# Final norm of a hybrid decoder layer on one core: the work of its last loop divided anew over VectorE, ScalarE and GpSimd

## What is computed

```python
def rmsnorm(x, g):
    xf = x.astype(jnp.float32)
    y = xf * lax.rsqrt(jnp.mean(xf * xf, -1, keepdims=True) + NORM_EPS)
    return (y * g.astype(jnp.float32)).astype(x.dtype)
...
# x: the residual stream, D_MODEL = 1024 wide; each token adds two weighted expert outputs,
# and the result goes through rmsnorm(x, final_norm_g)
```

## Time and profile before

| what | value |
|---|---|
| median of three runs | 1878.3 us |
| the profiled execution's own time | 1877.61 us |
| its span, first to last instruction | 1875.9 us |
| busy share of the span: PE, DVE, ACT, POOL | 88%, 35%, 20%, 10% |
| last expert step's scatter issued | 1824.90 us |
| first add of the last loop | 1833.22 us |
| last multiply of the last loop issued | 1872.33 us |

### The profile page before, as it was taken

How to read it: one execution, slowest core, us unless ns; L and a number is a source line. 1 busy time by engine, 2 the same in 40 slices (tenths; PEclk the granted TensorE clock), 3 DMA queues, 4 the chain that set the end, 5 groups by cost and what they waited for, 6 DMA issues and landing times.

```text
span 1875.9 us, 21634 instructions
## 1 busy us (share of the span) xinstructions
PE 1657.0 (88%) x8136; PEld 1060.9 (57%) x8136; DVE 661.6 (35%) x1238; ACT 369.1 (20%) x653; POOL 189.2 (10%) x297
## 2 busy tenths in 40 slices
PE   5999889999599989989989999999999758968960
PEld 3666556776277767767767775666445733323320
DVE  2003039734444343343433531677112311101117
ACT  3100230021113223133231325100012111101102
POOL 2003500002110110101101010000000001101100
PEclk9999979979699999999999999999999569989985
DMA  4111101109111111101111112265201076675646
GB/s 155 34 35 43 37 12 35 44 11 96 59 33 44 42 44 44 46 31 42 49 39 46 46 56 84 94 255 204 81 34 57 1 314 250 244 292 181 218 163 271
DMA packets 38072, 181.21 MB, mean 97 GB/s; under 512 B 5401, under 2 KB 5721, under 8 KB 29025
## 3 DMA queue, kind: packets, MB, share of 16 engines
q1 hardware_dynamic: 21808, 113.94, 17.7%
q0 software_dynamic: 16176, 66.01, 10.9%
HBM read 336.75 MB, written 38.21 MB: 200 GB/s over the span
## 4 chain that ended last, share of the span: by engine, by line
PE 83%; DMA 6%; DVE 5%; issue 3%; ACT 2%; SPq 0%; POOL 0%; DVEq 0%; ACTq 0%; POOLq 0%
PE ps L447 34%; PE ps L829 7%; PE ps L775 7%; PE ps L744 6%; PE ps L843 3%; DMA arena<-in_w_gu 3%; PE ps L689 3%; PE ps L603 2%; PE ps L598 2%; PE ps L581 2%; PE ps L608 2%; DMA scr<-h_rows,idx 1%; PE ps L497 1%; PE ps L790 1%; PE ps L465 1%
## 5 line engine op out<-in xcount | busy, mean ns | idle before, releaser
L447 PE MATMUL ps<-arena,wring 128*128 128x344 f32 x2304 | 699.6, 454 | 1.2 <-ACT arena L925 1.2
L447 PEld LDWEIGHTS ps<-arena,wring 128*128 128x128 f32 x2304 | 426.1, 190 | 205.5 <-issue 7.3
L829 PE MATMUL ps<-arena,scr 128*32 128x512 f32 x1280 | 152.1, 628 | 23.9 <-DMA arena<-in_w_gu 23.9
L1669 POOL DMA_DIRECT2D gate_scratch<-stage x96 | 52.0, 542 | 803.1 <-ACT stage L978 544.6
L775 PE MATMUL ps<-arena 128*128 128x512 f32 (+1 forms) x288 | 125.6, 594 | 1.2 <-DVE arena L1437 1.2
L744 PE MATMUL ps<-arena,wring 128*128 128x344 f32 x384 | 111.2, 451 | 0.0
L829 PEld LDWEIGHTS ps<-arena,scr 128*32 128x32 f32 x1280 | 41.6, 115 | 120.0 <-issue 102.4
L744 PEld LDWEIGHTS ps<-arena,wring 128*128 128x128 f32 x384 | 72.5, 189 | 38.6
L843 PE MATMUL ps<-arena,scr 128*32 128x512 f32 x640 | 77.6, 628 | 15.0 <-issue 13.6
L775 PEld LDWEIGHTS ps<-arena 128*128 128x128 f32 (+1 forms) x288 | 50.7, 178 | 71.0 <-issue 69.2
L886 ACT ACTIVATE arena<-ps 128x344 f32 (+1 forms) x63 | 28.8, 457 | 260.3 <-PE ps L447 242.8
(11 more groups left out here) (385 smaller groups left out, 1918.3 us busy)
## 6 DMA issues: line engine op xcount, KB each, us to landing
arena<-in_w_gu SPq DMA_DIRECT2D x160, 1024.0 KB
arena<-in_w_dn SPq DMA_DIRECT2D x80, 1024.0 KB
wring<-in_w_all SPq DMA_DIRECT2D x61, 512.0 KB, 3.8
gate_scratch<-stage POOLq DMA_DIRECT2D x96, 172.0 KB, 2.2
arena<-gate_scratch POOLq DMA_DIRECT2D x4, 2064.0 KB, 9.6
scr<-gate_scratch POOLq DMA_DIRECT2D x4, 2064.0 KB, 10.0
arena<-y_rows SPq DMA_DIRECT2D x16, 512.0 KB, 9.5
scr<-in_x_t SPq DMA_DIRECT2D x2, 2064.0 KB, 11.8
```

What stands on the lines that cost most here:

```text
L447: mm = pe.matmul(ps[:, c, 0:CW], wring[:, slot, k, :], H[:, k, chunk(c)], start=k == 0, stop=k == KT - 1)
L829: mm = pe.matmul(ps[S * j:S * (j + 1), i % 2, :], XT[i % 2][:, k * P + S * j:k * P + S * (j + 1)], GU[j][:, k * 2 * HID:(k + 1) * 2 * HID] ...
L1669: pool.dma_start(gate_scratch[:, bass.ds(base + g, 1), chunk(c)], stage[:, c:c + 1, :]).then_inc(sem(f"gate_out{c}"), 16)
```

## The change

The final norm no longer uses `norm_row`, which keeps the norm ahead of the experts alone and with the same instructions. For each tile n:

- VectorE makes its two adds. Between them it forms mean and epsilon of tile n-1 (`mean_square`), and after them the reciprocal of tile n-1 (`inverse`). It makes no multiply of a whole tile any more. The order of its instructions is: first add of n, mean of n-1, second add of n, reciprocal of n-1.
- ScalarE squares tile n as before, then multiplies tile n-1 in place by its reciprocal root (`scaled`, an activation with the per-row scale), then takes the root for tile n. 
- GpSimd multiplies tile n by the norm's weights into `YB`, one `tensor_tensor` of 128x1024, after it has waited for the scaled tile and, from the fourth on, for the output buffer.
- The SP queue stores as before.

The new steps need the semaphores `comb0`, `rs_r` and `y_sc`. To have them free, seven others are folded into existing ones: waits elsewhere name another semaphore with a shifted count (`norm_var` into `h_ready`, `k_sq` and `glu` into `lora_act`, `dec_p` and `dec_q` into `dec_act`, `dec_lm` into `rw_pre`, `xs_pre` into `ssm_h`). Each such wait is still for the same instruction's completion.

```diff
             for k in range(KT):
-                pe.wait_ge(sem("h_ready"), k + 1)
+                pe.wait_ge(sem("h_ready"), k + 2)
...
-                pe.wait_ge(sem("k_sq"), t + 1)
+                pe.wait_ge(sem("lora_act"), t + 3)
...
@@ ScalarE
+            def scaled(n):
+
+                m = rows_of(n)
+                act.wait_ge(sem("rs_r"), n + 1)
+                A(X2[0:m, n, :], X2[0:m, n, :], ACT.Copy, scale=RSTD[0:m, n:n + 1]).then_inc(sem("y_sc"), 1)
+
             for n in range(NTT):
                 m = rows_of(n)
                 act.wait_ge(sem("comb"), n + 1)
                 act.wait_ge(sem("row_sq"), NTT + n)
                 A(STG[0:m, 0:D], X2[0:m, n, :], ACT.Square, accum_out=SS[0:m, n:n + 1]).then_inc(sem("row_sq"), 1)
+                if n:
+                    scaled(n - 1)
                 act.wait_ge(sem("rs_v"), NTT + n + 1)
                 A(RSTD[0:m, n:n + 1], RSTD[0:m, n:n + 1], ACT.Sqrt).then_inc(sem("rs_s"), 1)
+            scaled(NTT - 1)
...
@@ VectorE
+            def mean_square(n):
+
+                m = rows_of(n)
+                dve.wait_ge(sem("row_sq"), NTT + n + 1)
+                ts(RSTD[0:m, n:n + 1], SS[0:m, n:n + 1], 1.0 / D, NORM_EPS, MUL, ADD).then_inc(sem("rs_v"), 1)
+
+            def inverse(n):
+
+                m = rows_of(n)
+                dve.wait_ge(sem("rs_s"), NTT + n + 1)
+                nc.vector.reciprocal(RSTD[0:m, n:n + 1], RSTD[0:m, n:n + 1]).then_inc(sem("rs_r"), 1)
+
             for n in range(NTT):
                 m = rows_of(n)
-                for c in range(2):
-                    dve.wait_ge(sem(f"yg_in{n}"), 32)
-                    r_ = X2[0:m, n, :]
-                    ins_ = stt(r_, YG[n][c][0:m, :], q1[5 + c][0:m, n:n + 1], r_, MUL, ADD)
-                    if c == 0:
-                        link(ins_)
-                    else:
-                        ins_.then_inc(sem("comb"), 1)
+                r_ = X2[0:m, n, :]
+                dve.wait_ge(sem(f"yg_in{n}"), 32)
+                stt(r_, YG[n][0][0:m, :], q1[5][0:m, n:n + 1], r_, MUL, ADD).then_inc(sem("comb0"), 1)
                 if n:
-                    norm_row(n - 1, NTT, 1, YB[(n - 1) % 3], "y_ready", [(f"y_out{(n - 1) % 3}", 16 * ((n - 1) // 3))] if n >= 4 else [])
-            norm_row(NTT - 1, NTT, 1, YB[(NTT - 1) % 3], "y_ready", [(f"y_out{(NTT - 1) % 3}", 16 * ((NTT - 1) // 3))])
+                    mean_square(n - 1)
+                dve.wait_ge(sem("comb0"), n + 1)
+                stt(r_, YG[n][1][0:m, :], q1[6][0:m, n:n + 1], r_, MUL, ADD).then_inc(sem("comb"), 1)
+                if n:
+                    inverse(n - 1)
+            mean_square(NTT - 1)
+            inverse(NTT - 1)
...
@@ GpSimd
+            for n in range(NTT):
+                m = rows_of(n)
+                pool.wait_ge(sem("y_sc"), n + 1)
+                if n >= 3:
+                    pool.wait_ge(sem(f"y_out{n % 3}"), 16 * (n // 3))
+                tt(YB[n % 3][0:m, :], X2[0:m, n, :], GAIN[0:m, 1, :], ALU.mult).then_inc(sem("y_ready"), 1)
```

More of the change, by code:

```diff
@@ L877, in _ @@
                 A(sq[:, k % 2, :], x_t[:, k, :], ACT.Square).then_inc(sem("norm_sq"), 1)
-            act.wait_ge(sem("norm_var"), 1)
+            act.wait_ge(sem("h_ready"), 1)
             inverse_root(RS0, RS0, "norm_std")
@@ L900, in _ @@
             for t in range(2):
-                A(TM[:, t, :], row(S_K + t), ACT.Square, scale=v("kkw", t)).then_inc(sem("k_sq"), 1)
+                A(TM[:, t, :], row(S_K + t), ACT.Square, scale=v("kkw", t)).then_inc(sem("lora_act"), 1)
             for t in range(2):
                 act.wait_ge(sem("evac"), 39)
-                A(row(S_CG + t), row(S_CG + t), ACT.Sigmoid).then_inc(sem("glu"), 1)
+                A(row(S_CG + t), row(S_CG + t), ACT.Sigmoid).then_inc(sem("lora_act"), 1)
             for n in range(4):
@@ L929, in _ @@
                 act.wait_ge(sem("bonus"), 2)
-                A(TM[:, t, 0:TP], LL[:, t, 0:TP], ACT.Exp, scale=-DECAY_SCALE).then_inc(sem("dec_p"), 1)
+                A(TM[:, t, 0:TP], LL[:, t, 0:TP], ACT.Exp, scale=-DECAY_SCALE).then_inc(sem("dec_act"), 1)
             A(smp[:, 5, :, :], smp[:, 5, :, :], ACT.Exp, scale=-DECAY_SCALE).then_inc(sem("pre_act"), 1)
             for t in range(2):
-                act.wait_ge(sem("dec_lm"), t + 1)
-                A(SG[:, t, 0:TP], SG[:, t, 0:TP], ACT.Exp, scale=-DECAY_SCALE).then_inc(sem("dec_q"), 1)
-                A(AA[:, t, 0:TP], LL[:, t, 0:TP], ACT.Exp, scale=DECAY_SCALE).then_inc(sem("dec_q"), 1)
+                act.wait_ge(sem("rw_pre"), t + 1)
+                A(SG[:, t, 0:TP], SG[:, t, 0:TP], ACT.Exp, scale=-DECAY_SCALE).then_inc(sem("dec_act"), 1)
+                A(AA[:, t, 0:TP], LL[:, t, 0:TP], ACT.Exp, scale=DECAY_SCALE).then_inc(sem("dec_act"), 1)
             gate_tile(0)
@@ L942, in _ @@
             A(smallv[:, 0:4], v("a_log", 0, 4), ACT.Exp).then_inc(sem("pre_act"), 1)
-            act.wait_ge(sem("xs_pre"), 1)
+            act.wait_ge(sem("ssm_h"), 2)
             A(XSS, XS, ACT.Sigmoid).then_inc(sem("pre_act"), 1)
@@ L1139, in _ @@
             dve.wait_ge(sem("pads"), 1)
-            dve.wait_ge(sem("h_ready"), KT)
+            dve.wait_ge(sem("h_ready"), KT + 1)
             nc.vector.tensor_copy(shift_out[:, :, :], PR[:, S_R:S_R + 7, PAD + TP - 1:]).then_inc(sem("shift_saved"), 1)
@@ L1171, in _ @@
             dve.wait_ge(sem("cum"), 2)
-            dve.wait_ge(sem("glu"), 2)
+            dve.wait_ge(sem("lora_act"), 6)
             for t in range(2):
@@ L1193, in _ @@
             for t in range(2):
-                tt(SG[:, t, 0:TP], LL[:, t, 0:TP], SG[:, t, 0:TP], SUB).then_inc(sem("dec_lm"), 1)
+                tt(SG[:, t, 0:TP], LL[:, t, 0:TP], SG[:, t, 0:TP], SUB).then_inc(sem("rw_pre"), 1)
             for t in range(2):
-                dve.wait_ge(sem("dec_p"), t + 1)
+                dve.wait_ge(sem("dec_act"), t + 1)
                 tt(row(S_R + t, 0, TP), row(S_R + t, 0, TP), TM[:, t, 0:TP], MUL)
@@ L1199, in _ @@
             for t in range(2):
-                dve.wait_ge(sem("dec_q"), 2 * t + 1)
+                dve.wait_ge(sem("dec_act"), 2 * t + 3)
                 tt(kk[:, t, :], kk[:, t, :], SG[:, t, 0:TP], MUL)
-                dve.wait_ge(sem("dec_q"), 2 * t + 2)
+                dve.wait_ge(sem("dec_act"), 2 * t + 4)
                 tt(bb[:, t, :], bb[:, t, :], AA[:, t, 0:TP], MUL)
                 tt(row(S_K + t, 0, TP), row(S_K + t, 0, TP), AA[:, t, 0:TP], MUL).then_inc(sem("rw_pre"), 1)
-            dve.wait_ge(sem("rw_pre"), 2)
+            dve.wait_ge(sem("rw_pre"), 4)
             dve.wait_ge(sem("pool_diff"), 2)
@@ L1220, in _ @@
             link(nc.vector.tensor_reduce(XS, XSW, AX, ADD))
-            tt(XS, XS, last(v("ssm_b", 0, 6), NSMP), ADD).then_inc(sem("xs_pre"), 1)
+            tt(XS, XS, last(v("ssm_b", 0, 6), NSMP), ADD).then_inc(sem("ssm_h"), 1)
             dve.wait_ge(sem("pre_act"), 1)
@@ L1439, in _, with norm_row @@
                                 ins_.then_inc(sem("merged"), 1)
-            def norm_row(n, base, gain, dst, sem_name, free):
+            def norm_row(n, dst, free):
                 m = rows_of(n)
                 rs = RSTD[0:m, n:n + 1]
-                dve.wait_ge(sem("row_sq"), base + n + 1)
+                dve.wait_ge(sem("row_sq"), n + 1)
                 ts(rs, SS[0:m, n:n + 1], 1.0 / D, NORM_EPS, MUL, ADD).then_inc(sem("rs_v"), 1)
-                dve.wait_ge(sem("rs_s"), base + n + 1)
+                dve.wait_ge(sem("rs_s"), n + 1)
                 link(nc.vector.reciprocal(rs, rs))
@@ L1450, in norm_row @@
                     dve.wait_ge(sem(name), value)
-                stt(dst[0:m, :], X2[0:m, n, :], rs, GAIN[0:m, gain, :], MUL, MUL).then_inc(sem(sem_name), 1)
+                stt(dst[0:m, :], X2[0:m, n, :], rs, GAIN[0:m, 0, :], MUL, MUL).then_inc(sem("h2_row"), 1)
             dve.wait_ge(sem("x_re"), 32)
@@ L1609, in _ @@
             nc.gpsimd.memset(PR[:, :, 0:PAD], 0.0).then_inc(sem("pads"), 1)
-            pool.wait_ge(sem("h_ready"), KT)
+            pool.wait_ge(sem("h_ready"), KT + 1)
             link(nc.gpsimd.memset(RESET, 1.0))
@@ L1672, in _ @@
             gate_store(0)
-            pool.wait_ge(sem("rw_pre"), 2)
+            pool.wait_ge(sem("rw_pre"), 4)
             pool.dma_start(SW, ins["wkv"]).then_inc(sem("states_in"), 16)
```

4 lines of the change are left out of this document (2 added, 2 removed).

## The result

The changed kernel took 1882.46 us by the median of 20 runs, against 1878.25 for the kernel before (20 runs). The measured ratio is 1.003, 95% interval 1.0016 to 1.0043 (the two medians alone give 1.0022). The interval leaves out 1, so the changed kernel is slower, by an amount at the edge of the 0.3% that the prediction counted as no change.

The account below looks back on a forecast made before the run. VectorE was taken as the bound, with three whole-tile passes per tile. Of 12.6 us saved, 11.4 come back as turns and the last tiles cost 3.4 more: 1878.3 + 2.2 = 1880.5 us, range 1871.5 to 1886.

Parts of the forecast that it names:

- Engines in turns: Last loop: VectorE's adds with two SBUF operands and GpSimd's multiplies exclude each other; chance of turns as forecast 0.62.
- The hold, 1.9 us: Last loop: each GpSimd multiply holds a VectorE add 1.9 us, 2.35 less 0.2 and some 0.2.
- Six adds held: Last loop: multiplies 0 to 5 hold one add each, 6 x 1.9 = 11.4 us, adds ending at 1868.8.
- Rival B: Last loop, slower: each multiply holds an add for its whole record plus handover, +4.9 to +9.0 us; chance 0.18.
- Multiply 3's wait for store 0, counted as 0: Last loop: store 0 lands near 1852.9, multiply 3 is ready at 1854.6, so no wait.
- 2.7 us a tile undisturbed: Last loop: VectorE without the multiply needs 2.7 us per tile against 4.35, a gain of 12.6 us.
- ScalarE's scaling, 1.04 us: Last loop: ScalarE's new scaling pass over 128x1024 takes 1.04 us; at twice that the loop loses 6 us.
- Rival C: Last loop: ScalarE's longer chain comes late, each small step waits, 0.3 us for each of 8 tiles; chance 0.07.
- GpSimd's multiply, 2.35 us: Last loop: GpSimd's multiply takes 2.35 us because its inputs lie a multiple of 8 apart; ends 1.92 and 2.80.
- The tail after the last add, 9.3 us: End of kernel: multiplies 6 to 8 in a row, 7.2 us, then last store 2.3; 9.3 against 5.9 before.
- Rival A: Last loop: engines run side by side with long instructions, adds stay 1.28 us; -6.3 us, 1872.0; chance 0.13.
- its mildest case (+4.9): Last loop: six holds of 2.35 us without handover, adds ending at 1871.5, span end 1880.8.

Follow-up runs that it names:

- experiment 1: Changed kernel without GpSimd's multiply, ScalarE scaling straight into the output buffer: 35.0 us from first add to end, against 47.9 in the changed kernel.
- (3): Changed kernel with GpSimd filling the output buffer with zeros instead of multiplying: 34.1 us from first add to end, every add 1.25 to 1.28 us.
- experiment 2: Changed kernel with expert rows left out, each add taking one operand from PSUM, multiplies kept: 39.5 us from first add to end.
- experiment 9: Changed kernel with ScalarE's scaled tiles in own buffers, 2 numbers over a multiple of 8 from the weights: 46.8 us first add to end, seven adds held.
- experiment 8: Changed kernel with ScalarE's scaled tiles in own buffers, 4 numbers over a multiple of 8 from the weights: 47.9 us from first add to end.
- Experiment 4: Kernel before, plus one 128x4 fill on GpSimd behind VectorE's last multiply: 47.1 us from first add to end, against 42.7.

## Why the prediction was right, and by how much of it

The forecast was no change that can be told, 1880.5 us, range 1871.5 to 1886. Measured were 1882.46 and a ratio whose interval reaches from 0.16% to 0.43%.

- **Engines in turns.** Shown. Removing the multiply, its reads, or one of VectorE's SBUF operands each ended the long adds (experiments 1, 3, 2), and a shorter multiply shortened them (9). The short rows of the recurrence were a sound sample of it.
- **The hold, 1.9 us.** It was 2.0. The cut of 0.4 that I made from 2.35 is 0.32 in the trace. The Trainium skill, page "SBUF — State Buffer", sections "SBUF: two separate sides" and "Who interferes with whom", makes the contention depend on two SBUF inputs on VectorE and on a GpSimd instruction that reads SBUF, not one that only writes it. The runs agree: one input in PSUM, no held add (experiment 2); a fill, no held add (3). An add is lengthened by less than the page's "for the whole instruction" would give if the instruction is its record: 2.0 of 2.35, 1.65 of 2.00. The records of the two engines overlap at both ends of a turn (multiply 0's ends at 1848.85 and the add it held at 1849.93, 1.08 us later, where a free add takes 1.28), so this does not say how long the reading side itself was kept.
- **Six adds held.** The count was right, the place wrong. The working had the first add of each tile from 3 to 8 held; the trace has both adds of tiles 3, 5 and 7 and none of the others. The delay of one hold makes the next multiply ready sooner in VectorE's order, so that multiplies come in pairs (1846.10 and 1848.93), and then VectorE runs free for a tile. Last add: 35.6 us after the first by the forecast, 35.5 in the trace. Rival B names the first add "of each tile from 2 to 8", which are seven, but its sum counts six as well.
- **Multiply 3's wait for store 0, counted as 0.** It was 0.67 us. The working put three holds before the end of tile 4's adds, where its own rule gives two, and the trace has two (1846.62 and 1849.96). In the changed kernel the wait moved no turn to another add, so it didn't show in the sum; in experiment 9 it did.
- **2.7 us a tile undisturbed.** 2.6 in experiment 1.
- **ScalarE's scaling, 1.04 us.** 1.13, still inside a tile, so nothing waited for it. Rival C is refuted: no reciprocal before the last tile waited over 0.2 us.
- **GpSimd's multiply, 2.35 us.** Right in size (2.33 to 2.37 where nothing holds it), by a rule that was wrong: 4 numbers off a multiple of 8 gave 2.34 us again (experiment 8), where the rule gave 1.92.
- **The tail after the last add, 9.3 us.** This is the step that failed. Up to the SP queue's end the trace has 9.0, as forecast; but the span ends 3.3 later (0.2 before), with GpSimd's drain. I had taken the last store's landing for the end of the program, as it is in the kernel before, and had not asked what a GpSimd that works to the last moment adds behind it. The closing instruction was in the trace of before, 6.4 us long, under work of others. Experiment 4 prices it at 3.3 us, the end points of the changed kernel at 3.1. With that the forecast's +2.2 becomes +5.3 to +5.5, against +5.2 in the loop. That the kernel still came out as no change is partly luck: with this term the loop stands 0.4 us under the 5.6 that the prediction took for the bound.

Rival A is refuted by adds of 3.3 us. Rival B, a hold of the whole record and a handover, is refuted by the same adds, for which its sign was 3.7 or longer; a result as slow as its mildest case (+4.9) came about through the drain instead.

## What to carry to other kernels

Before a pass is moved to GpSimd beside a busy VectorE, look at where VectorE's operands lie. With two in SBUF, a pass that costs VectorE 1.28 us itself held it for 2.0 from GpSimd, and the move lost; the small steps laid between the adds, which came with it, were worth 0.4 us a tile by themselves. Ask also what each engine does after its last instruction: one more instruction on GpSimd at the end of the program, a fill of 0.10 us, moved the end 3.3 us further behind the last store. And when a loop gets faster, look at the next wait in it: here the store of tile 0, which took back what the first four tiles had gained until there were more buffers.

## What the runs showed of the hardware that I had not expected

- GpSimd's closing drain ended 5.2 us after its last instruction in every kernel profiled here: behind a scatter, a multiply, and a fill of 128x4 numbers.
- A two-input pass of GpSimd over 128x1024 numbers took 2.33 to 2.39 us or 1.99 to 2.00 us, with where its inputs lay: moving one of them by one number at a time gave a pattern that repeats every 4 numbers. The rule behind it is open. A pass over 8 rows took as long as one over 128 (2.33).
- A VectorE instruction that is held counts as busy. VectorE's busy time in the last loop was 35.6 us in the changed kernel with 18 passes of a tile, and 36.0 in the kernel before with 27.
